# A hybrid encoder layer on one Trainium2 core: the skip term's scaling moves from VectorE to ScalarE in the chunk stage, and one weight unit is loaded earlier

## What is computed

```python
def ssd_chunked(x, dt, A, B, C):
    acs = jnp.cumsum(dt * A, axis=2)
    xdt = x * dt[..., None]
    seg = acs[:, :, :, None] - acs[:, :, None]
    Lmat = jnp.exp(jnp.where(tril[:, :, None, None], seg, -jnp.inf))
    cb = jnp.einsum('bcign,bcjgn->bcijg', C, B)
    y_diag = jnp.einsum('bcijg,bcijgh,bcjghp->bcighp', cb, Lmat, xdt)
    ...
    y_off = jnp.einsum('bcign,bcghpn->bcighp', C, h_prev) * jnp.exp(acs)[..., None]
    return (y_diag + y_off)...
...
y = ssd_chunked(forward) + flip(ssd_chunked(backward))
y = y + d_skip[:, None] * xs
y = y * silu(z)
y = y * rsqrt(mean(y * y) + EPS) * norm_g
```

## Time and profile before

| | us |
|---|---|
| median of 3 runs | 1792.2 (1790.76 to 1797.99) |
| the profiled execution's own time | 1789.94 |
| its span, first to last instruction | 1788.1 |
| TensorE busy | 1679.0 (94%) |
| VectorE busy | 906.0 (51%) |
| ScalarE busy | 592.5 (33%) |
| GpSimd busy | 410.8 (23%) |

### The profile page before, as it was taken

How to read it: one execution, slowest core, us unless ns; L and a number is a source line. 1 busy time by engine, 2 the same in 40 slices (tenths; PEclk the granted TensorE clock), 3 DMA queues, 4 the chain that set the end, 5 groups by cost and what they waited for, 6 DMA issues and landing times. The chain is left out here.

```text
span 1788.1 us, 26258 instructions
## 1 busy us (share of the span) xinstructions
PE 1679.0 (94%) x10034; PEld 1384.6 (77%) x10035; DVE 906.0 (51%) x991; ACT 592.5 (33%) x1017; POOL 410.8 (23%) x285
## 2 busy tenths in 40 slices
PE   7999999999999989999989999997899999996997
PEld 7878888877877767777878887885777777784786
DVE  5202777202134137742899226224768889941674
ACT  5211222231111136642344335113544443443332
POOL 1011111111211101003200121000356565652330
PEclk9999999999999999999789999998999999998999
DMA  6211222323456312017865434234767778733452
GB/s 224 78 54 60 80 79 80 107 84 115 133 182 191 103 66 66 28 52 241 255 198 140 165 124 139 82 95 172 253 219 271 274 285 305 283 129 141 142 188 94
DMA packets 117130, 267.17 MB, mean 149 GB/s; under 512 B 13027, under 2 KB 60851, under 8 KB 117036
## 3 DMA queue, kind: packets, MB, share of 16 engines
q1 hardware_dynamic: 101068, 211.08, 36.0%
q0 software_dynamic: 8320, 30.43, 5.2%
q10 hardware_dynamic: 7648, 24.35, 3.8%
HBM read 194.27 MB, written 71.55 MB: 149 GB/s over the span
## 5 line engine op out<-in xcount | busy, mean ns | idle before, releaser
L2224 DVE TENSOR_TENSOR ex_wlo<-ex_raw,ex_whi 128x1024 fp32r<-128x1024 f32 x102 | 162.2, 1591 | 10.6 <-ACT ex_whi L2218 7.3
L2802 PE MATMUL rt_p<-ex_whi,ex_xh 128*128 x280 | 113.6, 406 | 15.6 <-DVE ex_wlo L2224 8.9
L2220 DVE CAST ex_whi<-ex_raw 128x1024 fp32r<-128x1024 f32 x96 | 107.8, 1123 | 40.3 <-DMA ex_raw<-experts 36.6
L271 PE MATMUL rest_p<-hi_h,whi_in 128*128 128x512 f32 (+1 forms) x480 | 121.2, 361 | 0.0
L271 PE MATMUL rest_p<-lo_h,whi_in 128*128 128x512 f32 (+1 forms) x480 | 119.6, 357 | 0.0
L271 PE MATMUL rest_p<-hi_h,wlo_in 128*128 128x512 f32 (+1 forms) x480 | 119.6, 357 | 0.0
L2804 PE MATMUL rt_p<-ex_whi,ex_xl 128*128 x280 | 109.9, 392 | 0.0
L2803 PE MATMUL rt_p<-ex_wlo,ex_xh 128*128 x280 | 109.7, 392 | 0.0
L271 PEld LDWEIGHTS rest_p<-hi_h,whi_in 128*128 128x128 f32 x480 | 79.7, 188 | 21.6 <-issue 7.6
L945 POOL TENSOR_TENSOR wlo_in<-wraw_in,whi_in 128x1024 fp32r<-128x1024 f32 x18 | 43.9, 2439 | 227.4 <-ACT whi_in L908 227.3
L914 ACT ACTIVATE rest_out<-rest_p 128x1024 f32<-128x1024 f32 x20 | 20.5, 1026 | 214.2 <-PE rest_p L271 210.6
(11 more groups left out here) (415 smaller groups left out, 3992.2 us busy)
## 6 DMA issues: line engine op xcount, KB each, us to landing
ex_raw<-experts SPq DMA_DIRECT2D x96, 512.0 KB, 6.2
wraw_in<-units SPq DMA_DIRECT2D x36, 512.0 KB, 4.2
y_slots<-ex_y ACTq DMA_DIRECT2D x35, 512.0 KB, 4.1
rest<-rest_out SPq DMA_DIRECT2D x20, 640.0 KB, 5.6
scan_e<-erow SPq DMA_DIRECT2D x32, 256.0 KB, 4.8
xtok<-conv_tok SPq DMA_DIRECT2D x10, 640.0 KB, 3.4
z_x<-x SPq DMA_DIRECT2D x10, 512.0 KB, 4.0
ao_gate<-rest SPq DMA_DIRECT2D x8, 640.0 KB, 5.9
```

The costliest lines, as they stand in the source:

```text
L271: mm = pe.matmul(out[:, n, 0:size], w[:, kk, :], h[:, kk, c:c + size], start=(kk == 0 and w is whi and h is hi), stop=(kk == ktiles - 1 an ...
L2220: eng.tensor_copy(self.hi[:, e % 2, n, :], self.raw[e % 2][:, n, :]).then_inc(self.w_hi[n], 1)
L2224: eng.tensor_tensor(self.lo[:, e % 2, n, :], self.raw[e % 2][:, n, :], self.hi[:, e % 2, n, :].bitcast(F32), ALU.subtract).then_inc(self.w ...
L2802: pe.matmul(gu[s][:, :], xh[s][:, kk, :], hi, start=(kk == 0), stop=False)
```

## The change

`weighted_x` leaves VectorE's queue. On ScalarE it becomes eight activations of 64 columns each, one per head, with the token's factor as the scale; they stand behind the two exponentials of the same unit and ahead of `root`. The waits are the same three as before (`same_step` for unit 0, `x_in` for group 0, `m_used` for the buffer). The load of the first next weight unit moves from chunk 2 to the start of `early`; the second stays. GpSimd now waits for one unit before it splits that unit, and not for both.

```diff
@@ load_chunk
             if t == 2:
                 sp.wait_ge(ao_mm, KT)
-                for n in range(2):
-                    sp.dma_start(next_raw[:, n, :], d["units"][U_SO + n]).then_inc(next_in, 16)
+                sp.dma_start(next_raw[:, 1, :], d["units"][U_SO + 1]).then_inc(next_in, 16)
@@ early
+            sp.dma_start(next_raw[:, 0, :], d["units"][U_SO]).then_inc(next_in, 16)
             params(sp)
             load_chunk(sp, 0)
@@ GpSimd
             same_token()
-            pool.wait_ge(next_in, 32)
             for n in range(2):
+                pool.wait_ge(next_in, 16 * (n + 1))
                 split_next(n, False)
                 split_next(n, True)
@@ ScalarE
+            def weighted_x(w):
+                t, g, s = w // 2, w % 2, w // 2 % 2
+                if w == 0:
+                    act.wait_ge(same_step, 9)
+                if g == 0:
+                    act.wait_ge(x_in[s], 32 * (t // 2 + 1))
+                if w >= 2:
+                    act.wait_ge(m_used, 4 * w - 7)
+                for j in range(HPG):
+                    h = g * HPG + j
+                    ins = act.activation(xw[g][:, j, :], xs[s][:, h * SSD_HEAD:(h + 1) * SSD_HEAD], ACT.Copy,
+                                         scale=same[:, t, h:h + 1])
+                ins.then_inc(xw_ready, 1)
...
             exp(0, 0)
             exp(0, 1)
+            weighted_x(0)
             for w in range(UNITS + 2):
...
                     exp(w + 1, 0)
                     exp(w + 1, 1)
+                if w + 1 < UNITS:
+                    weighted_x(w + 1)
                 if 1 <= w <= UNITS:
                     root(w - 1)
@@ VectorE
-                dve.tensor_tensor(xw[g][:, :, :], xs[s][:, g * 512:(g + 1) * 512].rearrange("p (h e) -> p h e", e=SSD_HEAD),
-                                  per_head(same[:, t, g * HPG:(g + 1) * HPG]), ALU.mult).then_inc(xw_ready, 1)
...
-            weighted_x(0)
...
                     carried_c(w + 1)
-                    weighted_x(w + 1)
```

More of the change, by code:

```diff
@@ L2064, in carried_c @@
                                   ).then_inc(c_ready, 1)
-            def weighted_x(w):
-                t, g, s = w // 2, w % 2, w // 2 % 2
-                if w == 0:
-                    dve.wait_ge(same_step, 9)
-                if g == 0:
-                    dve.wait_ge(x_in[s], 32 * (t // 2 + 1))
-                if w >= 2:
-                    dve.wait_ge(m_used, 4 * w - 7)
-                dve.tensor_tensor(xw[g][:, :, :], xs[s][:, g * 512:(g + 1) * 512].rearrange("p (h e) -> p h e", e=SSD_HEAD),
-                                  per_head(same[:, t, g * HPG:(g + 1) * HPG]), ALU.mult).then_inc(xw_ready, 1)
             def merge(w, p):
```

## The result

The changed kernel took 1799.43 us in the median (1790.4 to 1810.1, 16 runs), the kernel before 1794.15 beside it (1790.76 to 1797.99, 16 runs): a ratio of 1.0034, 95% interval 1.0021 to 1.0047, so some 6 us slower. The same program run again gave 1.0023 (1.0009 to 1.0036), some 4 us. 3.3 us faster was forecast; both the sign and the range missed.

What follows compares the result with a forecast made beforehand. VectorE (5.94 us a unit) was taken as the first limit, TensorE (5.38) close behind, SyncE's queue (12.65 for two units) from 906 us. Terms +0.4 - 3.7 - 0.6 + 1.8 - 1.2 = -3.3 gave 1788.9 us, range 1781 to 1794.

Steps and rivals of the forecast that it cites:

- One split less in the middle: Chunk 2, units 6 and 7: one GpSimd split fewer slows VectorE there; -3.7 us, bounds 2.7 and 4.7.
- the ring: Two-chunk loop: state landing, ScalarE and VectorE to `carried_c`, SyncE's next load; landing to `carried_c` 6.0 us, forecast 6.9.
- The start: Stage start: the earlier load costs its issue, +0.4 us; the split moved beside units 0 to 2 costs nothing.
- The fallback price: Stage start: if the cover for the moved split is gone, `carried_c` of unit 0 is held up some 2.1 us.
- the start pays: Rival, stage start: first split or earlier load holds up unit 0 by 2.1 us; total -1.2, 1791.0 us; chance 0.15.
- The loop: Chunks 4 to 9: ScalarE's added work delays `carried_c` by 0.9 us at each of two bindings; +1.8 us.
- -0.6: Between `carried_c` of units 6 and 7: VectorE's unit is shorter by one instruction; one unit's gain, -0.6 us.
- -1.2: Stage end, unit 17 to unit 19: VectorE runs without gaps and gains two units' worth, -1.2 us.
- SyncE as the second limit: From 906 us: SyncE's queue needs 12.65 us for two units, more than TensorE's 10.76.
- ScalarE becomes the late one at every chunk: Rival, each landing: TensorE's skip product stalls 2.3 us and its clock falls; +6.9, 1799.1 us; chance 0.12.

Runs made afterwards that it cites:

- e11: Kernel before with the scaling moved to ScalarE, loads and splits left as before, h on its own semaphore, four row transfers a chunk instead of eight: ratio 0.9920.
- e2: Kernel before with only the early load and early split of the first next weight unit, scaling still on VectorE: ratio 1.0007.
- e5: The changed kernel run and profiled again, nothing altered: ratio 1.0023 against the kernel before.
- e13: Kernel before with the first next weight unit loaded early, but both units split in chunk 2: ratio 1.0015.
- e1: Kernel before with only the scaling moved to ScalarE, both weight units loaded and split in chunk 2 as before: ratio 1.0011.
- the first profile: The first profiled execution of the changed kernel, against the kernel before: 1808.62 us, one of its long executions.
- e15: Kernel before with only the scaling moved to ScalarE, the eight activations of group 0 done twice: ratio 1.0062 against the kernel before.
- e7: Kernel before with four row transfers of two rows each a chunk instead of eight: ratio 0.9953.
- e3: The changed kernel with h on a semaphore of its own, so the scaling waits for x only: ratio 0.9977 against the kernel before.

## Why the prediction was wrong, step by step

**The prices were right.** The eight activations take 2.02 us, 2.0 was forecast from rows of other shapes; VectorE's unit is 5.34 us where nothing else is late (e11). The skip product waits for ScalarE 2.5 us in three times, at most the microsecond each that was allowed.

**One split less in the middle: by itself worth a little more than forecast, but not kept in the changed kernel.** -3.7 was forecast, -4.7 at best. In e2 the longest unit beside the split went from 13.8 to 9.2 us, -4.6, and the whole stretch to gate 6 from 47.2 to 41.7, -5.5. In the changed kernel the longest unit is still 14.6 us (12.7 in e5), and the stretch is only 3.2 us shorter (2.7): the ring takes part of it back already there.

**The start: wrong, +0.4 for what measures +4.2 in e2 and +3.4 in the changed kernel.** Two steps failed there. The early load was priced at its issue, 0.43 us; with it the first gate comes 1.8 us later (e13). And the first split was put at nothing, because VectorE is busy only 14.96 of 23 us there. But the mean over a window hides that `weigh`, `carried_c` and `weighted_x` of the first units stand in one chain with nothing ahead of them to cover a delay: 2.4 us (e2 against e13). The fallback price that the prediction named, 2.1, was nearly what came. The prediction also left out that `same` is made from the loads behind the new one, and that on ScalarE the scaling of unit 0, with the exponentials of unit 1 behind it, waits for `same` (e5). The rule on SBUF that the prediction cites from the Trainium skill ("SBUF — State Buffer", section "Who interferes with whom") agrees with 2.80 us for the `carried_c` of 1.22. Of the rivals, "the start pays" had the place but half the price.

**The loop: wrong in size and, more, in what it meant.** The prediction saw the ring and gave it +0.9 for each of two passages, beside -0.6 and -1.2 for VectorE. A passage cost 7.44 - 6.03 = 1.4 us instead of 0.9, and there are more than the two that were counted: behind 906 us SyncE starts its load within 0.03 us of such a `carried_c` three times in e1 and in the first profile, four times in e5. Three times 1.4 are 4.2 us, beside the 3.9 by which e1's late stretch grew. What a passage cost beyond 0.9 is the `weigh` that waits 0.55 us for an exponential: ScalarE does square, copy and exponential behind the split, and these were late too; I had counted only root and split. The graver error is the frame. Where a ring sets the time, work taken from an engine outside its path is worth nothing, and each passage's price comes in full, without the savings ahead of it and behind. VectorE's 0.60 a unit couldn't be cashed, in the tail either (the last two gates are 4.8 us apart in e5 and 3.3 in e1, 2.7 before). Gates 6 to 19 grew by 3.9 us in e1 and 7.4 in e5, where the three terms together (-0.6 + 1.8 - 1.2) came to nothing. e15 gives the slope: 9 us for 2.05 us of work in the ring.

**SyncE as the second limit: seen, and not carried through.** The first part of the prediction says that SyncE's queue needs 12.65 us for two units; it should have followed that VectorE at 11.9 could gain next to nothing behind 906 us. e7 shows it: 3 us less of issues a chunk are worth 8.4 us without any engine doing less.

**The rival with the slower side had the size by chance, not the place.** "ScalarE becomes the late one at every chunk" said 1799.1, and 1799.4 came, but it said so through TensorE's skip product and its clock. The clock did fall, from 0.94 to 0.86, and at the landing of 920.51 TensorE's 16 products take 1.98 us as they did before; but e3 has the same 0.86 and is faster than the kernel before, e3 and e15 move the time by what stands between landing and `carried_c`, and TensorE's skip product waits for ScalarE only 2.5 us in all. With the ring open the clock is 0.97 (e7, e11). What the lower clock costs by itself was not measured.

**What stays open.** Of the early load's 1.8 us SyncE's queue shows 1.4; why the issue of `scan_gain` grows behind it, and where the other 0.4 comes from, was not separated. And the two halves sum to 3.3 us with intervals of some 3 us either way, neither told from nothing by itself, so whether they also hurt each other can't be said from the times; by the traces the late stretch of the changed kernel (+7.4 and +10.6) is longer than those of both halves together (+3.9 and +1.3).

## What to carry to other kernels

Before crediting work moved off the fullest engine, look for a ring through the loads: from a landing over the engines to the semaphore for which the queue that issues the next load waits, and back. If each engine on that way stands idle until the one before it releases it, only what stands in the ring counts, also on an engine that is half idle; shorten it (here by fewer issues and a semaphore for each transfer) and the same move pays 6 us, where it gained nothing before. Work moved to a stage's start isn't hidden because the window there is half idle: ask which chain ends last there.

## What the runs showed of the hardware

An issue on SyncE costs about the same for one row as for two: mostly 0.60 us for each of the eight row transfers, 0.49 to 0.54 for each of the four. Four issues fewer a chunk were worth 8.4 us of the kernel. The Trainium skill ("DMA: Bandwidth & Descriptors", section "Rules for kernel authors") advises to coalesce many small transfers; e7 agrees, here for the issuing queue's sake. And the wait for two transfers at one semaphore costs as much as the later of them: once x had a semaphore of its own, ScalarE could start 1 to 2 us earlier after the issues, and the changed kernel was 8 to 10 us faster (e3).
